# One weight array with one 512 KB load per unit, and a beginning that takes units of two chunks in turn

## What is computed

```python
h = x + 0.5 * swiglu(rms_norm(x, g), w_gate, w_up, w_down)   # D_MODEL 1024, D_FF 2816
# rms_norm: x * rsqrt(mean(x*x) + eps) * g
# swiglu:   (silu(u @ w_gate) * (u @ w_up)) @ w_down
```

## Time and profile before

| | us |
|---|---|
| median of three runs (lowest to highest) | 1215.43 (1215.17 to 1215.56) |
| the profiled execution's own time | 1215.56 |
| its span, first to last instruction | 1213.7 |
| PE busy in the span | 1203.9 (99%) |
| ACT, DVE, POOL busy | 690.9, 774.8, 73.6 |
| granted TensorE clock, mean | 1.000 |

### The profile page before, as it was taken

How to read it: one execution, slowest core, us unless ns; L and a number is a source line. 1 busy time by engine, 2 the same in 40 slices (tenths; PEclk the granted TensorE clock), 3 DMA queues, 4 the chain that set the end, 5 groups by cost and what they waited for, 6 DMA issues and landing times.

```text
span 1213.7 us, 17135 instructions
## 1 busy us (share of the span) xinstructions
PE 1203.9 (99%) x5673; PEld 991.4 (82%) x5673; DVE 774.8 (64%) x1087; ACT 690.9 (57%) x1009; POOL 73.6 (6%) x123
## 2 busy tenths in 40 slices
PE   8999999999999999999999999999999999999998
PEld 6888888877788888888888788888888887888887
DVE  5665556697775665557668666665556666655554
ACT  5655545575555555547675566655555546655543
POOL 2320000000000000000220110000000001000000
PEclk9999999999999999999999999999999999999999
DMA  9977764644456999764655417986655554776771
GB/s 303 253 208 219 225 197 139 190 141 156 151 180 204 238 244 242 232 167 160 185 166 188 153 62 240 238 235 202 204 168 162 168 157 148 213 221 202 221 225 44
DMA packets 209089, 232.01 MB, mean 191 GB/s; under 512 B 55888, under 2 KB 150224, under 8 KB 209040
## 3 DMA queue, kind: packets, MB, share of 16 engines
q1 hardware_dynamic: 164784, 214.81, 56.9%
q10 hardware_dynamic: 42464, 10.81, 5.2%
q0 software_dynamic: 1792, 5.75, 2.0%
HBM read 219.78 MB, written 1.05 MB: 182 GB/s over the span
## 4 chain that ended last, share of the span: by engine, by line
PE 95%; ACT 1%; DVE 1%; DMA 1%; POOL 1%; issue 0%; SPq 0%; POOLq 0%
PE bank L1937 30%; PE bank L1939 29%; PE bank L1938 29%; PE bank L1993 2%; PE bank L2170 1%; PE bank L2186 1%; PE bank L2157 1%; DMA sb_gates<-h_xT 1%; PE bank L2155 0%; DMA sb_raw<-e_w_in 0%; ACT sb_probs L1212 0%; ACT sb_wh L720 0%; POOL sb_gates L606 0%; PE bank L2032 0%; PE bank L2474 0%
## 5 line engine op out<-in xcount | busy, mean ns | idle before, releaser
L1937 PE MATMUL bank<-sb_wh,sb_aTh 128*128 128x512 f32 (+1 forms) x1132 | 439.6, 388 | 1.6 <-DVE sb_wl L1295 1.6
L1939 PE MATMUL bank<-sb_wh,sb_aTl 128*128 128x512 f32 (+1 forms) x1132 | 434.3, 384 | 0.0
L1938 PE MATMUL bank<-sb_wl,sb_aTh 128*128 128x512 f32 (+1 forms) x1132 | 433.9, 383 | 0.0
L1295 DVE TENSOR_TENSOR sb_wl<-sb_raw,sb_wh 128x1024 fp32r<-128x1024 f32 x271 | 327.7, 1221 | 102.6 <-ACT sb_wh L720 98.3
L720 ACT ACTIVATE sb_wh<-sb_raw 128x1024 fp32r<-128x1024 f32 (+1 forms) x273 | 285.9, 1054 | 114.0 <-PE bank L1939 42.5
L1937 PEld LDWEIGHTS bank<-sb_wh,sb_aTh 128*128 128x128 f32 x1132 | 212.8, 188 | 43.9 <-issue 3.4
L1939 PEld LDWEIGHTS bank<-sb_wh,sb_aTl 128*128 128x128 f32 x1132 | 212.7, 188 | 42.6
L1938 PEld LDWEIGHTS bank<-sb_wl,sb_aTh 128*128 128x128 f32 x1132 | 213.0, 188 | 40.0
L1295 DVE TENSOR_TENSOR sb_wl<-sb_z,sb_wh 128x1024 fp32r<-128x1024 f32 x132 | 160.2, 1233 | 37.9 <-ACT sb_wh L720 37.8
L720 ACT ACTIVATE sb_wh<-sb_z 128x1024 fp32r<-128x1024 f32 x132 | 137.0, 1056 | 59.2 <-PE bank L1939 42.1
L1937 PE MATMUL bank<-sb_wh,sb_hTh 128*128 128x512 f32 x320 | 125.0, 391 | 0.0
(11 more groups left out here) (224 smaller groups left out, 913.4 us busy)
## 6 DMA issues: line engine op xcount, KB each, us to landing
sb_raw<-w_in SPq DMA_DIRECT2D x80, 256.0 KB, 3.0
sb_z<-ffn_w_down SPq DMA_DIRECT2D x64, 256.0 KB, 4.4
sb_z<-w_down SPq DMA_DIRECT2D x64, 256.0 KB, 3.7
sb_raw<-w_gate SPq DMA_DIRECT2D x54, 256.0 KB, 3.4
sb_raw<-w_up SPq DMA_DIRECT2D x54, 256.0 KB, 4.1
sb_raw<-ffn_w_gate SPq DMA_DIRECT2D x53, 256.0 KB, 3.6
sb_raw<-ffn_w_up SPq DMA_DIRECT2D x53, 256.0 KB, 4.5
sb_raw<-e_w_in SPq DMA_DIRECT2D x40, 256.0 KB, 3.0
```

What stands on the lines that cost most here:

```text
L1295: dve.tensor_tensor(wl[:, u % NSPLIT, :], raws[SLOT[u]], wh[:, u % NSPLIT, :].bitcast(F32), ALU.subtract).then_inc(low_done, 1)
L1937: pe.matmul(dst, lh, w_hi, start=start, stop=False)
L1938: pe.matmul(dst, lh, w_lo, start=False, stop=False)
L1939: return pe.matmul(dst, ll, w_hi, start=False, stop=stop)
```

## The change

Four things are changed.

**One array.** The host packs all weights into one array `h_units` of 404 x 128 x 1024 float32, in the order in which PE takes them (`weight_units`). Each unit is loaded by one DMA of 512 KB, with rows of 4 KB. The eight small columns `wf` become an array of their own.

**The order of the first eight units.** Unit 1 is now the first gate/up unit of chunk 1 (k-tiles 0-1); chunk 0 has units 0, 2, 3, 4 and chunk 1 has 1, 5, 6, 7 (`FRONT`). Units 0 and 1 both come in four DMAs of 128 KB and are multiplied by halves (`early_unit`). The hidden transposes stand before unit 7 (they stood before the third unit of chunk 1).

**The order of the first loads.** xT comes in five pieces: k-tile 0 (ACT's queue), k-tile 1 (in the middle of unit 0), 2-3, 4-5, 6-7, each of the last three ahead of units 2, 3, 4. ACT's queue brings first only the 8 columns of gains; the other vectors come later on SP's. x in token order comes behind unit 5, ahead of unit 6.

**The sum of squares.** It is made by `token_ssq` on ACT from x in token order, between the splits of units 5 and 6. The squares of xT, POOL's additions, the eight matmuls and DVE's copy are gone.

```diff
+FRONT = [(0, 0), (1, 0), (0, 1), (0, 2), (0, 3), (1, 1), (1, 2), (1, 3)]
...
+            def load_unit(u, c=0):
+                free_raw(u, c)
+                at = u if isinstance(c, int) and c == 0 else u + 6 * c
+                sp.dma_start(raws[SLOT[u]].unsqueeze(1), units[bass.ds(at, 1)].rearrange("u p n -> p u n"))\
+                    .then_inc(loaded[SLOT[u]], 16)
...
+            def load_front():
+
+                load_early_unit(0)
+                load_early_unit(1)
+                for u in range(2, 5):
+                    load_xt(u, 2 * u - 2, 2 * u)
+                    load_unit(u)
+                load_unit(5)
+                sp.dma_start(ident[:], d["c_ident"]).then_inc(ident_in, 16)
+                sp.dma_start(vecs[:, KT:NCOL], d["h_vecs"][:, KT:NCOL]).then_inc(vecs_in, 16)
+                for t in range(NT):
+                    sp.dma_start(x[:, t, :], xv[:, t, :]).then_inc(x_in, 16)
+                for u in range(6, 10):
+                    load_unit(u)
+
+            def load_early_unit(u):
 
                 for k in range(2):
-                    for g in range(2):
-                        sp.dma_start(raw[:, 0, 512 * k + FC * g:512 * k + FC * g + FC], ffn_w[0][g][:, k, 0:FC])\
-                          .then_inc(first_loaded if k == 0 else loaded[0], 16)
+                    for a in (512 * k, 512 * k + FC):
+                        sp.dma_start(raws[u][:, a:a + FC], units[u, :, a:a + FC])\
+                          .then_inc(first_loaded[u] if k == 0 else loaded[u], 16)
+                    if u == 0 and k == 0:
+                        load_xt(1, 1, 2)
...  POOL
-            for h in range(2):
-                a = h * KT * T // 2
-
-                pool.wait_ge(xsq_done, h + 1)
-                link(pool.tensor_tensor(xsq[:, a:a + 2 * T], xsq[:, a:a + 2 * T], xsq[:, a + 2 * T:a + 4 * T], ALU.add))
-                pool.tensor_tensor(xsq[:, a:a + T], xsq[:, a:a + T], xsq[:, a + T:a + 2 * T], ALU.add).then_inc(xsq_added, 1)
...  ACT, in ffn
                 split(u + 1)
+                if f == 0:
+
+                    act.wait_ge(x_in, 32)
+                    token_ssq(norm, x)
+                    split(u + 2)
                 rstd_known(norm)
 
-                act.wait_ge(units_used, u + 4)
+                act.wait_ge(units_used, u + 4 if f > 0 else u + 5)
                 silu_step(0, FFN_FIRST_BANK[f])
-                splits(u + 2, 2)
+                if f > 0:
+                    split(u + 2)
+                split(u + 3)
                 ht_step(1, hTh[:, :, :])
...  ACT, the beginning (LEAD is 4, so split(2 - LEAD) is unit 2)
+            act.wait_ge(gain_in, 16)
+            for k in range(2):
+                first_xt_high(k, k, k + 1)
+                early_split(0, k)
+            for k in range(2):
+                early_split(1, k)
+            first_xt_high(2, 2, 4)
             split(2 - LEAD)
-            first_squares(0)
+            first_xt_high(3, 4, 6)
             split(3 - LEAD)
-            first_squares(1)
+            first_xt_high(4, 6, KT)
             ffn(0)
...  DVE, the beginning
+            for k in range(2):
+                first_xt_low(k)
+                early_split(0, k)
+            for k in range(2):
+                early_split(1, k)
             first_xt_low(2)
             first_xt_low(3)
-            split(1 - LEAD)
-            for k in range(4, KT):
-                first_xt_low(k)
-            splits(2 - LEAD, 2)
+            split(2 - LEAD)
+            first_xt_low(4)
+            first_xt_low(5)
+            split(3 - LEAD)
+            first_xt_low(6)
+            first_xt_low(7)
...  PE
                 if f == 0:
-                    first_unit()
-                    chunk(u, FFN_FIRST_BANK[f], a_ready(norm), begun=1)
-                    sum_squares()
+                    early_unit(0, FFN_FIRST_BANK[f])
+                    early_unit(1, 0)
+                    chunk(u + 1, FFN_FIRST_BANK[f], a_ready(norm), begun=1)
 
                     pe.wait_ge(ident_in, 16)
+                    gate_up(0, lambda: transpose_hidden(0), 3, 1)
                 else:
                     chunk(u, FFN_FIRST_BANK[f], a_ready(norm), before={1: lambda: xt_half(norm, 1)})
-
-                gate_up(0, lambda: transpose_hidden(0))
+                    gate_up(0, lambda: transpose_hidden(0))
```

More of the change, by code:

```diff
@@ L470, in load_gate_up @@
[L470 to L482 removed]
+            units = d["h_units"]
@@ L728, in split @@
                         return
-                act.wait_ge(loaded[SLOT[u]], 32 * NTH[u] + 32 * c)
+                act.wait_ge(loaded[SLOT[u]], 16 * NTH[u] + 16 * c + (16 if SLOT[u] < 2 else 0))
                 if u >= NSPLIT:
@@ L750, in xt_high @@
                     xt_high_pair(norm, g)
-            squares = [NT]
+            squares = [0]
             def junk_free():
@@ L1392, in ffn @@
                 if f == 0:
-                    first_sums()
+                    split(u + 2)
                 mul_step(0, FFN_FIRST_BANK[f])
-                splits(u + 2, 2)
+                if f > 0:
+                    split(u + 2)
+                split(u + 3)
                 ht_step(0, hTl[:, :, :], hTh[:, :, :])
@@ L2038, in down, with gate_up @@
                                     wh[:, u_slot % NSPLIT, w], wl[:, u_slot % NSPLIT, w], start, stop)
-                def gate_up(c, halfway=None):
-                    for i in range(4):
-                        if i == 2 and halfway is not None:
-                            halfway()
+                def gate_up(c, before=None, at=2, begun=0):
+                    for i in range(begun, 4):
+                        if i == at and before is not None:
+                            before()
                         square(u + 4 + i, 2 * i, aTh, aTl, 0, i == 0, i == 3, c)
@@ L2559, in k_tiles, with weight_units, put, square @@
 def k_tiles(a):
     return a.reshape(-1, P, a.shape[-1]).transpose(1, 0, 2)
+def weight_units(inputs):
+    units = np.empty((TOTAL, P, UNIT), np.float32)
+    filled = [0]
+    def put(tiles):
+        units[filled[0]] = tiles.reshape(P, UNIT)
+        filled[0] += 1
+    def square(w, k0, n0):
+        put(k_tiles(w)[:, k0:k0 + 2, n0:n0 + 512])
+    def chunk(w, n0):
+        for k in range(0, w.shape[0] // P, 2):
+            square(w, k, n0)
+    def ordered(w, order):
+        for n, g in order:
+            square(w, 2 * g, 512 * n)
+    def quarters(w):
+        for kq, h in QUARTERS:
+            put(k_tiles(w)[:, 4 * kq:4 * kq + 4, 256 * h:256 * h + 256])
+    def ffn(gate, up, down):
+        both = np.stack([k_tiles(gate), k_tiles(up)], axis=2)
+        down = k_tiles(down)
+        def gate_up(c):
+            for i in range(4):
+                put(both[:, 2 * i:2 * i + 2, :, FC * c:FC * c + FC])
+        if filled[0] == 0:
+            for c, i in FRONT:
+                put(both[:, 2 * i:2 * i + 2, :, FC * c:FC * c + FC])
+        else:
+            gate_up(0)
+            gate_up(1)
+        for c in range(1, NFC):
+            if c > 1:
+                gate_up(c)
+            for k in range(2):
+                put(down[:, 2 * (c - 1) + k])
+        for k in range(2):
+            put(down[:, 2 * (NFC - 1) + k])
+    w = {name: inputs[name][0] for name in ("ffn1_w_gate", "ffn1_w_up", "ffn1_w_down", "w_in", "w_branch_sb",
+                                            "w_branch_moba", "w_out", "ffn2_w_gate", "ffn2_w_up", "ffn2_w_down",
+                                            "e_w_in_2", "e_w_out_2", "o_w_in_2", "o_w_out_2")}
+    wq, wkv, wo = (inputs[f"xa_{name}_2"] for name in ("wq", "wkv", "wo"))
+    gate, up, down = (inputs[f"w_{name}_2"] for name in ("gate", "up", "down"))
+    ffn(w["ffn1_w_gate"], w["ffn1_w_up"], w["ffn1_w_down"])
+    for n0 in W_IN_COLS:
+        chunk(w["w_in"], n0)
+    for n in range(2):
+        chunk(w["w_branch_sb"], 512 * n)
+    ordered(w["w_branch_moba"], OUT_MOBA)
+    ordered(w["w_out"], OUT_8)
+    ffn(w["ffn2_w_gate"], w["ffn2_w_up"], w["ffn2_w_down"])
+    chunk(wkv[0], 0)
+    chunk(wkv[0], 512)
+    for n0 in E_IN_COLS:
+        chunk(w["e_w_in_2"], n0)
+    chunk(wkv[1], 0)
+    chunk(wkv[1], 512)
+    ordered(w["e_w_out_2"], OUT_8)
+    quarters(wq[0])
+    ordered(wo[0], OUT_4)
+    ffn(gate[0], up[0], down[0])
+    for n0 in O_IN_COLS:
+        chunk(w["o_w_in_2"], n0)
+    ordered(w["o_w_out_2"], OUT_8)
+    quarters(wq[1])
+    ordered(wo[1], OUT_4)
+    ffn(gate[1], up[1], down[1])
+    assert filled[0] == TOTAL
+    return units
```

193 lines of the change are left out of this document (47 added, 146 removed).

## The result

The change made the kernel slower by 3.15 us, 0.26%. The whole interval of the ratio lies above 1. The forecast was 1211.9.

The account below looks back on a forecast made before the run. PE bounds the kernel, busy 1203.9 of 1213.7 us, with 4.19 us lost in the beginning. Gains 4.4 minus costs 0.9 make net 3.5, so 1211.9 us; own range 1211.2 to 1212.9, whole range 1210.8 to 1214.0.

Parts of the forecast that it names:

- the single DMA at 0: Later units: one 512 KB DMA each halves SP's issues, off PE's path; effect 0, bounds -0.4 and +0.4 us.
- rival C: Three-slot stages: single loads make PE wait once a flight takes 5.6 us; 1215.5 to 1217; chance 0.09 with similar losses.
- Unit 2: term 0.5: Beginning: unit 2 lands at 10.1, starts at 12.64, 0.5 us lost; landing 9.7 gives 0.1, 11.0 gives 1.4.
- The rule of the landing: Early loads: a landing trails its bytes; ACT could use a piece 1.35 us after its bytes had flowed.
- x: forecast 18.1 to 19.2: Before unit 6: x lands then, ACT's squares follow; 0.1 us lost, bounds 0 and 1.5 (x at 20.4).
- Rival A: Before unit 6: x is late, the rest holds; x at 20.8 stalls PE 2.0 us, time 1213.8; chance 0.15.
- the row of 401: Trace of before, 19 to 23 us: 401 GB/s with 2 and 4 KB rows; at that rate x lands at 18.1.
- PE's start: gain 0.2: First real matmul: gains and xT come first, start about 6.2, warm-up until 6.37; gain 0.2 us, bounds 0 and 0.4.
- The 2.11 of the sum of squares: Before unit 4: loss from POOL's additions and eight small matmuls with their restart; 2.11 us forecast to go.
- Before down unit 8: Transposes before unit 7 leave one unit, not two, as cover; 0.3 us lost, bounds 0.1 and 0.6.
- rival D: Before the transposes: PE is held for the factor and the 2.11 us come back; needs x beyond 19.4 by over 1 us.
- one and the same lead beyond 40 us: Every landmark beyond 40 us is earlier by 3.5 us; a growing or shrinking lead means the single loads matter.

Follow-up runs that it names:

- e1: The kernel before with its own beginning, and from unit 10 on one 512 KB DMA per unit in rows of 4 KB: 1218.07 us, ratio 1.0017.
- e12: The changed kernel with another order of the first loads, early pieces contiguous in HBM, unit 2 seventh on SP's queue, later rows still 4 KB: 1214.54 us, ratio 0.9995.
- e3: The changed kernel with, from unit 10 on, still one 512 KB DMA per unit but in rows of 1 KB: 1215.04 us, ratio 0.9994.
- e8: The changed kernel with, from unit 10 on, one 512 KB DMA per unit in rows of 2 KB: 1214.53 us, ratio 0.9992.
- e2: The changed kernel's beginning, with the old loads from unit 10 on (two 256 KB DMAs, rows of 1 or 2 KB): 1215.99 us, ratio 1.0000.
- e5: e3 with nine filler matmuls on zeros between units 1 and 2, where PE otherwise idles: 1213.84 us, ratio 0.9985.

## Why the prediction was wrong

- **The step that failed first: "all off the path while PE waits for no load", the single DMA at 0, bounds -0.4 and +0.4.** The rows of 4 KB cost 2.5 us alone (e1) and 2.6 to 2.9 in another setting (e12). I looked for what the new loads would do to the units themselves, as in rival C, and a single load was harmless there: a 512 KB load into sb_raw takes 3.9 us from issue to landing in the profile after, into sb_z 4.6, under the 5.6 from which C decides. (The 3.2 us that rival C works out by the Trainium skill's "DMA: Bandwidth & Descriptors", section Anatomy of one DMA, was not met; that fit is given there for DMAs issued from GpSimd, and these are SP's.) I didn't look at who else uses the DMA engines. The 36 transposes on ACT's queue stood in the trace of before, the longest at 10.2 us with 11 of cover. So the overlap was wrong: PE waits for no load, but it waits for a transpose that shares the DMA engines with the loads, 2.54 us at 415. One DMA for each unit in rows of 1 or 2 KB costs nothing (e3, e8).
- **Unit 2: term 0.5, bounds 0.1 to 1.4; measured 2.3 (a wait of 2.07 and the restart).** This is most of why 1.5 us and not 3.5 were won by down unit 8. The rule of the landing held (2.1 MB had flowed at 10.8, and the unit was used 1.35 later); the rate did not. I took the 243 GB/s up to 8.90 over to a list of ten small DMAs: SP's issues follow one another at 0.46 to 0.52 us, so pieces of 128 KB from its queue can bring 250 to 285 GB/s at most, and pieces with 1 KB rows 4 or 8 KB apart flow at 135 to 149. The bound of 11.0 for the landing named this danger and was too narrow by 1.15.
- **The clock.** No term, no rival. I counted a wait by its length; in part of the executions a wait was followed by a slow stretch, worth 1.6 to 2.2 us in e3 and e2. After has two waits of over 2 us and a median 2.3 over its profiled execution. That the 2.3 are this is argued from e5 and from the clocks of the executions; a filler in the kernel after itself was not run. The rival, a transpose held up longer in other executions than in the profiled one, is open, since e1 and e12 spread by 3 to 5 us at a clock of 1.000.
- **x: forecast 18.1 to 19.2, measured 20.4, cost 0.** Rival A did not come, because the gap before unit 2 moved PE back by about as much; with unit 2 in time, x at 20.4 would have cost the 1.5 us of the prediction's own bound. From 12 to 20 the rate was 406 GB/s, so the row of 401 was the right one to go by. The 358 that the Trainium skill's "DMA: Bandwidth & Descriptors", section Where 436 GB/s comes from, gives as the HBM limit of a core was not a bound for this kernel, which runs on one core; its section Measured gives that figure as each core's share when both cores of an HBM domain stream.
- **PE's start: gain 0.2, bounds 0 and 0.4; measured 0.** It came 0.24 earlier, at 6.38, but the first two matmuls then took 0.99 from start to start, where before they took 0.70 (6.62 to 7.32). Unit 0 ended at 9.66, before at 9.60. The prediction had read these two by their lengths (0.87) and not by their starts, against its own rule.
- **What held.** PE steps from 6.38 to the end of unit 1 without a gap (1.82 won). The 2.11 of the sum of squares went. Before down unit 8 stood a wait of 0.22, 0.45 with its restart (forecast 0.3, bounds 0.1 and 0.6). DMA moved 398 GB/s between 10 and 20 (forecast over 380). Units 3 to 6 waited for nothing, and rival D did not come. I forecast one and the same lead beyond 40 us and named its change as the sign that the single loads matter; that sign came, at 415.

## What to carry to other kernels

Before the shape of a large stream of loads is changed, list what else travels over the same DMA engines (transposes, small loads on other queues) and how much cover each has: here rows of 4 KB in one queue held up the other's transfer, though PE waited for none of the loads themselves. At the start of a kernel count issues and bytes separately, try the early pieces contiguous in HBM, and let the first unit that PE will miss stand early in its queue. A wait of PE of about 2 us should be priced with what may follow it, and not only by its length. And compare the profiled execution with the spread of the others before its trace is taken for the cause of the whole difference: here it showed 0.9 of 3.15 us.
